# A bias row's wait, an attention lead-in, token statistics and two weight blocks are rearranged in a two-layer transformer kernel

## The reference, cut to what matters

```python
# hybrid layer
h = modulate(rms_norm(x, norm1_w), sh1, sc1)
p = h @ w_in                                   # q, k, v, z, xs, b, c
attn = neighbourhood_attention(q, k, v, kc, vc, rpb, rows)   # q, k rotated (axial_rope)
y_ssd, _, _ = ssd_bidirectional(...)
x = x + g1 * (concat([attn, y_ssd]) @ w_out)
x = x + g2 * conv_glu(modulate(rms_norm(x, norm2_w), sh2, sc2), ...)
# second layer: attention with a bucketed relative bias, then a GLU,
# each with a norm before and a norm after:
#   x = x + post * rms(attention(...) @ w_o);  x = x + post * rms(glu(...) @ w_out)
```

## Time and profile before

| what | value |
|---|---|
| three runs | 1469.12 us median (1468.83 to 1469.87) |
| profiled execution | 1470.08 us, its span 1468.3 us |
| TensorE busy | 94% of the span, granted clock 0.969 |
| VectorE, ScalarE, GpSimd busy | 39%, 40%, 43% |
| chain that ended last | TensorE 84%, GpSimd 5%, VectorE 4%, ScalarE 3% |
| transfers | 165.55 MB, mean 113 GB/s |

### The profile page before, as it was taken

One profiled execution on the slowest core, in us unless ns is written; L12 is line 12 of the kernel. 1 busy time (PEld: TensorE's weight loads), 2 busy tenths in 40 slices (PEclk: granted clock), 3 DMA queues, 4 the chain that ended last, 5 costly groups with the idle time before them and its releaser, 6 DMA issues.

```text
span 1468.3 us, 17191 instructions
## 1 busy us (share of the span) xinstructions
PE 1376.2 (94%) x6306; PEld 1099.9 (75%) x6306; DVE 572.7 (39%) x1080; ACT 583.6 (40%) x897; POOL 626.0 (43%) x516
## 2 busy tenths in 40 slices
PE   8989999896788799999999989899979999999997
PEld 1778878785676688888888878655768888888885
DVE  2655623677823634444334352467060000001113
ACT  3513444672312544344322443477353322322331
POOL 0232324337614354444465754333514454454563
PEclk9999999999889899999999989999989999999999
DMA  9226575000013244554433322200201322222221
GB/s 393 101 87 244 215 185 180 6 30 1 1 58 143 86 191 181 202 198 171 172 144 114 137 93 86 86 1 1 87 29 58 114 86 93 107 86 96 105 86 58
DMA packets 26984, 165.55 MB, mean 113 GB/s; under 512 B 2688, under 2 KB 4992, under 8 KB 8496
## 3 DMA queue, kind: packets, MB, share of 16 engines
q1 hardware_dynamic: 24912, 150.11, 28.1%
q10 hardware_dynamic: 2016, 14.68, 2.6%
HBM read 162.65 MB, written 6.32 MB: 115 GB/s over the span
## 4 chain that ended last, share of the span: by engine, by line
PE 84%; POOL 5%; DVE 4%; ACT 3%; issue 2%; DMA 1%; SPq 0%; ACTq 0%; DVEq 0%; POOLq 0%
PE bank L271 51%; PE bank L335 9%; PE bank L312 5%; PE bank L1203 3%; PE bank L668 2%; PE bank L648 2%; PE bank L521 2%; POOL arena L846 1%; POOL w_lo L264 1%; PE bank L1176 1%; DMA w_raw<-w_dram 1%; PE bank L510 1%; POOL arena L848 1%; PE bank L658 1%; PE bank L498 1%
## 5 line engine op out<-in xcount | busy, mean ns | idle before, releaser
L264 POOL TENSOR_TENSOR w_lo<-w_raw,w_hi 128x512 fp32r<-128x512 f32 x352 | 471.3, 1370 | 652.9 <-ACT w_hi L255 652.9
L271 PE MATMUL bank<-h_hi,w_hi 128*128 128x512 f32 x1120 | 445.4, 398 | 16.0 <-POOL w_lo L264 8.1
L271 PE MATMUL bank<-h_lo,w_hi 128*128 128x512 f32 x1120 | 439.7, 393 | 0.0
L271 PE MATMUL bank<-h_hi,w_lo 128*128 128x512 f32 x1120 | 439.6, 392 | 0.0
L255 ACT ACTIVATE w_hi<-w_raw 128x2048 fp32r<-128x2048 f32 x89 | 170.5, 1916 | 365.9 <-PE bank L271 189.6
L271 PEld LDWEIGHTS bank<-h_hi,w_hi 128*128 128x128 f32 x1120 | 213.0, 190 | 61.7 <-issue 13.7
L271 PEld LDWEIGHTS bank<-h_hi,w_lo 128*128 128x128 f32 x1120 | 212.6, 190 | 45.3
L271 PEld LDWEIGHTS bank<-h_lo,w_hi 128*128 128x128 f32 x1120 | 212.9, 190 | 43.6
L2081 DVE TENSOR_TENSOR arena<-arena,bank 128x512 f32 (+1 forms) x22 | 15.1, 688 | 210.2 <-PE bank L271 210.2
L1953 DVE TENSOR_TENSOR h_lo<-arena,h_hi 128x1024 fp32r<-128x1024 f32 x22 | 32.7, 1502 | 136.9 <-ACT h_hi L1630 125.4
L1797 DVE SCALAR_TENSOR_TENSOR arena<-bank,params,arena 128x511 f32<-128x511 f32 (+1 forms) x36 | 25.4, 705 | 140.6 <-ACT arena L1610 114.6
(11 more groups left out here) (263 smaller groups left out, 1859.4 us busy)
## 6 DMA issues: line engine op xcount, KB each, us to landing
w_raw<-w_dram SPq DMA_DIRECT2D x92, 1024.0 KB, 4.8
ada_ring<-ada_dram SPq DMA_DIRECT2D x30, 1024.0 KB, 4.8
ada_ring<-ada_dram ACTq DMA_DIRECT2D x14, 1024.0 KB, 5.2
arena<-ada_dram SPq DMA_DIRECT2D x4, 1024.0 KB, 9.7
arena<-x_dram SPq DMA_DIRECT2D x2, 2048.0 KB, 11.7
bias_copies<-bias_rows SPq DMA_DIRECT2D x1, 4096.0 KB, 28.0
arena<-bias_copies SPq DMA_DIRECT2D x1, 3072.0 KB, 14.7
out_dram<-arena SPq DMA_DIRECT2D x8, 256.0 KB, 2.1
```

Of the source, the lines that this page charges most:

```text
L264: last = nc.gpsimd.tensor_tensor(w_lo[b % 2][:, part], w_raw[b % 2][:, part], w_hi[b % 2][:, part], ALU.subtract)
L271: last = nc.tensor.matmul(bank[:, :], w[:, ft, k, :], x[:, k, :], start=k == first and m == 0, stop=k == final and m == 2)
```

## The change

Four places are touched.

1. TensorE's wait for `brow_sb` moves from ahead of tile 4 to the first group of transposes, after tile 8.
2. Group 1's inverse sum and maxima go ahead of the last rotation on VectorE. ScalarE's first copy out of a transpose then waits for that rotation (`tile_free` 24). ScalarE rounds block 13 after its attention turn 3 and not after tile 23. The rest of block 13 is made by VectorE in turns 5, 7, 9 and 11 and not by GpSimd.
3. ScalarE takes the statistic of token block t+1 ahead of the one of the summed row t, and VectorE does the same: `normalise_row` is cut in two.
4. Block 90 is set aside too: its rounding and its split no longer wait for block 88 to be read. The squares of the last four token blocks go to another scratch place.

```diff
-A_ASIDE = {57: 0, 58: 4096, 91: 8192}
+A_ASIDE = {57: 0, 58: 4096, 90: 8192, 91: 12288}
...
-        over = sb("arena_rounded", [P, 12288], F32R)
+        over = sb("arena_rounded", [P, 16384], F32R)
...
-        XRT, XN, turn_sum, junk = A(A_XRT, 4, D), A(A_XN, 4, D), A(A_TURN, 2, D), A(A_JUNK, 2, 512)
+        XRT, XN, turn_sum = A(A_XRT, 4, D), A(A_XN, 4, D), A(A_TURN, 2, D)
+        junk, junk_end = A(A_JUNK, 2, 512), A(A_HID, 2, 512)
...
             def copy(G, odd):
                 u = 2 * G + odd
                 act.wait_ge(s["ptr"], u + 1)
+                if u == 0:
+                    act.wait_ge(tile_free, 24)
...
                 if G >= 2:
                     out_low(G - 2)
+                if G in (5, 7, 9, 11):
+                    q = (G - 5) // 2
+                    if q == 0:
+                        dve.wait_ge(hi_done, B_OUT + 2)
+                    part = slice(q * 512, q * 512 + 512)
+                    last = nc.vector.tensor_tensor(w_lo[1][:, part], w_raw[1][:, part], w_hi[1][:, part], ALU.subtract)
+                    if q == 3:
+                        last.then_inc(lo_done, 1)
...
-                if u in (6, 10, 14, 18):
-                    q = (u - 6) // 4
-                    if q == 0:
-                        pool.wait_ge(hi_done, B_OUT + 2)
-                    part = slice(q * 512, q * 512 + 512)
-                    last = nc.gpsimd.tensor_tensor(w_lo[1][:, part], w_raw[1][:, part], w_hi[1][:, part], ALU.subtract)
-                    if q == 3:
-                        last.then_inc(lo_done, 1)
...
-            low(pool, 90)
+            low_aside(pool, 90)
             low_aside(pool, 91)
...
                 if k == 0:
                     pe.wait_ge(tile_free, 8)
+                    pe.wait_ge(brow_sb, 1)
...
-            pe.wait_ge(brow_sb, 1)
             for n in range(4, 23):
...
-                if n % 2:
+                if n % 2 and n < 23:
                     high(act, n // 2 + 2)
...
-            attention1_act(act, range(1, NG + 2))
+            attention1_act(act, range(1, 4))
+            high(act, B_OUT + 1)
+            attention1_act(act, range(4, NG + 2))
...
-            for t in range(4):
+            y_statistic(0, 0)
+            for t in range(1, 4):
                 y_statistic(t, t)
-                x_statistic(t)
+                x_statistic(t - 1)
+            x_statistic(3)
...
-            high(act, B_DOWN2 + 9)
+            high_aside(act, B_DOWN2 + 9)
...
-                if kind != "v":
+                if kind != "v" and n < 23:
                     dve.wait_ge(half_used, n + 1)
...
+                    if j == 3:
+                        attention1_dve(dve, range(1, 2))
                     rope(bank, q1[:, j], 0.125, j)
...
-            attention1_dve(dve, range(1, NG + 2))
+            attention1_dve(dve, range(2, NG + 2))
...
-            def normalise_row(t):
+            def right_square(t):
                 dve.wait_ge(add_right, t + 1)
...
+
+            def normalise_row(t):
                 dve.wait_ge(x_root, t + 1)
...
                 add_row(t, t, prow[0])
-                normalise_row(t)
+                if t:
+                    normalise_row(t - 1)
+                right_square(t)
+            normalise_row(3)
```

More of the change, by code:

```diff
@@ L124, in build @@
         sb("arena_start", [P, A_OVER])
-        over = sb("arena_rounded", [P, 12288], F32R)
-        sb("arena_end", [P, ARENA - A_OVER - 12288])
+        over = sb("arena_rounded", [P, 16384], F32R)
+        sb("arena_end", [P, ARENA - A_OVER - 16384])
         def view(tensor, at, *dims):
@@ L1724, in y_statistic @@
             def y_statistic(q, t):
+                squared = junk if q < 4 else junk_end
                 for h in range(2):
@@ L1727, in y_statistic @@
                     col = 2 * t + h
-                    nc.scalar.activation(junk[:, h, :], ps[col][:, :], ACT.Square, accum_out=y_part[:, col:col + 1]).then_inc(o_sq, 1)
+                    nc.scalar.activation(squared[:, h, :], ps[col][:, :], ACT.Square, accum_out=y_part[:, col:col + 1]).then_inc(o_sq, 1)
                 act.wait_ge(o_sq, 2 * q + 2)
```

## The result

The changed kernel takes 1449.91 us in the median of four runs (1447.50 to 1450.99), the kernel before 1468.97 us beside it. The ratio is 0.9867 [0.9850, 0.9884]: 19.1 us faster. The forecast was 16.1 us faster; the result lies at the lower edge of its range, and just outside it when the ratio is applied to the first median (0.9867 x 1469.12 = 1449.6). The profiled execution took 1449.60 us, its span 1447.8, with a granted clock of 0.975 (before 0.969).

The account below looks back on a forecast made before the run. TensorE, busy 94% of the span, was taken as the bound, so only its stops and slow-clock stretches pay. Gains of 6.8 + 2.5 + 1.7 + 5.1 = 16.1 us gave 1453.0 us, range 1449.8 to 1456.8.

Parts of the forecast that it names:

- Cost nothing: Attention loop: block 13's four splits moved from GpSimd to VectorE cost nothing; 4 x 0.2 = 0.8 us without ScalarE's cover.
- the token statistics' term: Token statistics in turns: block 3's transposes start earlier, 1.7 us gained, between 0.8 and 2.6.
- The bias row: Tile 4: removing the 4.1 us stop and 2.7 us slow stretch gains 6.8 us; 4.1 if the clock stayed down.
- the 6 us of room: Tile 6: GpSimd ends block 3's rest at 96.3, TensorE needs it at about 102.5, so no new wait.
- The lead-in: Attention's start: group 0 weighed earlier, 3.1 us gained, bounds 2.2 and 3.8; 2.5 after the rounding's loss.
- the rounding: Block 13's rounding between attention turns 3 and 4: 0.6 us lost, between 0 and 1.15.
- The rival that the lead-in gives nothing: Attention's start: TensorE at 1.2 GHz and rounding's whole 1.15 us cancel the gain; 1455.5 us, chance 0.14.
- The rival that VectorE and GpSimd meet in the loop: Attention loop: each of four splits costs up to 1.4 us through port contention, 5.6 in all; 1458.6 us, chance 0.04.
- The last blocks: Blocks 90 and 91: the 3.3 us stop and 1.8 us slow stretch go, 5.1 us; 3.3 if the clock dips.
- The sum: Whole kernel: 6.8 + 2.5 + 1.7 + 5.1 = 16.1 us faster, median 1453.0 us.
- the bounds: Whole kernel: gains of 9.2 to 18.3 us, so times of 1459.9 to 1450.8 us.
- The slower rival: Attention loop stays at 1.2 GHz, each turn costing 4.4 us more; 1506 us over twelve turns, chance 0.02.

Follow-up runs that it names:

- e7_pool_split: Changed kernel with block 13's four splits back on GpSimd instead of VectorE: 1454.29 us, ratio 0.9887.
- e13_pad_split: e7_pool_split plus four tiny one-column VectorE writes that nobody reads, in attention turns 5, 7, 9 and 11: 1449.84 us, ratio 0.9864.
- e14_pool_split_again: e7_pool_split run once more without any edit: 1452.32 us, ratio 0.9883.
- e15: Kernel before with only four tiny unread VectorE writes added, in attention turns 5, 7, 9 and 11: 1466.21 us, ratio 0.9980.
- e1_bias: Kernel before with only TensorE's wait for the bias row moved: 1462.71 us, ratio 0.9957.
- e8_bias_fill: Kernel before, bias row's wait kept in place, with 18 unread TensorE products ahead of it: 1466.48 us, ratio 0.9979.
- e16_after_pad: Changed kernel with four more tiny unread VectorE writes: 1448.22 us, ratio 0.9861.
- e3_stat: Kernel before with only the token statistics taken in turns: 1467.15 us over twelve runs, ratio 0.9982.
- e5_after_again: Changed kernel run once more without any edit: 1449.51 us, ratio 0.9865.
- e6_fill: Changed kernel with unread TensorE products in three gaps, at the attention's start and in the token statistics: 1445.91 us, ratio 0.9842.
- e10_fill_again: e6_fill run once more without any edit: 1448.08 us, ratio 0.9855.
- e11_fill_stat: Changed kernel with unread TensorE products in the token statistics alone: 1448.83 us, ratio 0.9857.
- e2_lead: Kernel before with only the attention's part: group 1's maxima earlier, block 13's rounding in the loop, its splits on VectorE: 1462.90 us, ratio 0.9957.
- e4_aside: Kernel before with only block 90 set aside: 1464.41 us, ratio 0.9968.
- e12_round_back: Changed kernel with block 13's rounding back behind the last projection tile: 1448.48 us, ratio 0.9855.

## Why the prediction was off

**Where it failed first: the splits, "Cost nothing".** In their own place they cost nothing: 0.69 us each, no turn longer, the attention the same in e7_pool_split and e13_pad_split. I asked only what the four instructions displace in their turns, and not what they do to VectorE's stream afterwards. They move its later instructions by 0.2 us against GpSimd's, and a meeting that cost GpSimd 1.0 us on the path now costs VectorE the same, off it. Behind it the clock does better: 1.4 to 1.5 us at the second layer's first norm, 0.5 to 1.3 in the statistics. In all 2.5 us (e13 against e14) to 3.1 us (e15 against before) by medians. Of the 3.0 us by which the forecast was off, this is most. That the four instructions bring all of it is shown; that the clock's share follows from the 1.0 us of the split is not. In e1_bias and e8_bias_fill the split takes 6.99 and 6.97 us as before, and yet the norm's stretch gave 2.8 and 1.6 us. What pauses VectorE wasn't measured; that its place moves with the number of instructions ahead is shown, and no row names another engine as its releaser (e16_after_pad's timeline has "issue" there, a wait for nothing that the profile shows). Why the clock is better at the norm and in the statistics isn't settled either.

**Where it failed next: the token statistics' term.** It read "1090.26 - 1088.7 = 1.6 us", with "TensorE, on the slow level as before", and I took 1.7, at best 2.6. The order was right to a tenth. The transposes of blocks 0 to 2 were forecast for 1085.75 in the time of before; they began at 1074.22 + 11.5 = 1085.7. The new order gave 2.0 us for 1.7 forecast (2.0 in e3_stat too). What the sum left out is what happens behind block 3's transposes. The chain of before had the slow lots of 1.09 and 2.56 us there, but I costed the slow stretch only for tile 4 and for the last blocks, and here held the level fixed. It moved: TensorE was back at 2.4 GHz before the first product, worth 2.0 us more. Having one stop for two doesn't explain that by itself, since e3_stat has the same order and the first lot at 1.08 and 2.22. Measured 4.0 in the changed kernel, 4.2 in e5_after_again and 4.0 in e13_pad_split, but 2.7 in e3_stat, e7_pool_split and e14_pool_split_again, which lack VectorE's four instructions; with the level held by unread products 4.8 to 4.9 in e6_fill, e10_fill_again and e11_fill_stat. So 1.0 us of the excess is this term's own, 0.3 by order and 0.7 by the clock, and the rest hangs on the effect above.

**The bias row: right.** 6.8 forecast, 6.6 measured, of which e8_bias_fill puts 2.4 (2.7 forecast) on the clock. GpSimd needed 7.46 us for block 3's split where I had counted 4.95, and came to 98.65 us: the 6 us of room shrank to about 4 and held.

**The lead-in: order right, clock low.** I took 3.1, halfway between 2.2 and 3.8, and 0.6 for the rounding. The order gave 3.8, the slow first weighing took 1.7 (1.4 estimated), the rounding 0.25: 1.8 where the sum had 2.5. The rival that the lead-in gives nothing is refuted; e2_lead and e6_fill start the weighing the whole 3.8 sooner and keep 3.4 and 3.3 of it to the attention's end. The rival that VectorE and GpSimd meet in the loop is refuted too, since no scaling ran beside a split; they met at another place, and to the change's advantage.

**The last blocks: right.** 5.1 forecast, 5.0 measured, here and in e4_aside. GpSimd was 1.5 us ahead of TensorE (1.9 forecast).

**The sum.** Without the remote effect the sum stands: e14_pool_split_again shows 16.4 us in its profiled run (8.3 up to the attention's end, 0.4, 2.7 and 5.0) for 16.1 forecast, and 17.0 by its median; e7_pool_split, the same code, shows 16.1 and 14.5. That it comes so near is partly luck, since the lead-in's 0.7 us too much and the statistics' 1.0 too little cancel. With the effect the changed kernel shows 20.5 and 19.1. The two profiled executions differ from their medians by 1.4 us of that (1470.08 is 1.1 above, 1449.60 is 0.3 below).

**What the range lacked.** Its lower end, 1449.8, lies 1.0 us under the 1450.8 of the bounds; the 0.3 us named for the launches belong to 1450.5. Unedited stretches differ by more: 3.0, 2.0, 2.5, 4.1, 3.1 and 3.3 us in six profiled runs of kernels with VectorE's splits (the first, e5_after_again, e6_fill, e10_fill_again, e11_fill_stat, e12_round_back). The kernel before reaches the good place at times by itself: beside e1_bias three of its 18 runs took 1464.87 to 1466.00 us at a clock of 0.972 to 0.975, the others 1468.25 to 1470.74 at 0.968 to 0.970. So do one of e7_pool_split's five runs (1448.04) and two of e3_stat's twelve.

The slower rival, the attention loop at 1.2 GHz, is refuted: the window from 262.3 to 269.8 us reads 1.00, and turns take 4.4 us.

## What to carry to other kernels

Where a stop of TensorE like the four here (3 to 6 us) goes, is shortened or merges with another, count the slow products behind it too, with both ends for them: the clock's share was 2.4 of 6.6 us at tile 4, 1.8 of 5.0 at the last blocks and up to 2.0 of 4.0 in the statistics; a stop that must stay can be filled with unread products, which gave another 5 us in three places here. Added or removed instructions on VectorE can move the time by some 3 us far from their place, so an edit costed at nothing keeps a margin of that size, and a few tiny instructions tell such an effect from the edit's own work.

## What the runs showed of the hardware

- The same instruction behind the same gap runs at either level in different launches. The first weighing behind 2.1 us of idling took 1.99 us in e2_lead, 2.80 in e5_after_again, 3.59 in the changed kernel and 3.68 in e11_fill_stat. The Trainium skill, TensorE: Matmul & The Clock Gate, section What's actually happening, says that the slow level is the default, that activity releases it, and that the moment of release varies from run to run. The traces agree on the last two (unread products brought 1.00 for 0.78 around the second norm, and the four times above), and add that a few such moments shift a stretch of this kernel by 1 to 3 us. On the default they show nothing: over the first 12 us of the changed kernel's span the profile reads 1.00.
- Products whose results nobody reads hold the clock as others do: 0.81 and 0.78 became 1.00 and 1.00 around the second norm, and 45 products took 10.93 us for 13.21.
- A difference of 0.2 us in VectorE's stream decides which of two engines waits 1.0 us. It was the same in every launch: 6.97 to 6.99 us for the split in seven traces, 5.99 to 6.00 in eleven.
- Four VectorE writes of one column each, read by nobody, made the kernel before 3.1 us faster.
